# Router products and token-row turns moved into the loop of the mixer's output projection, with the norm applied per token at its end

## The reference, cut to what matters

```
def modulate(h, shift, scale):
    return h * (1.0 + scale) + shift
...
        x = x + g1 * mix
        h = modulate(rmsnorm(x, p['norm_ffn'][l]), sh2, sc2)
        x = x + g2 * hierarchical_moe(h, p['router_group_w'][l], p['router_group_b'][l],
...
    g_logits = (t @ wg + bg).astype(jnp.float32)
    g_idx = jnp.argmax(g_logits, axis=-1)
    e_logits = (jnp.einsum('nd,dge->nge', t, we) + be).astype(jnp.float32)
    e_val, e_idx = lax.top_k(e_in_group, TOP_K_IN_GROUP)
```

## Time and profile before

| | |
|---|---|
| median of 3 runs | 1279.28 us (1276.4 to 1279.57) |
| profiled execution, its own time | 1278.2 us |
| its span | 1276.4 us, 14669 instructions |
| TensorE busy | 1094.6 us (86%) |
| VectorE busy | 470.9 us (37%) |
| ScalarE busy | 257.2 us (20%) |
| GpSimd busy | 185.9 us (15%) |
| mean granted TensorE clock | 0.932 |
| read from and written to DRAM | 333.22 and 30.11 MB |

### The profile page before, as it was taken

The page is one execution under the profiler, slowest core; times in us unless marked ns, Lnnn a source line. Parts: engine busy times, 40 slices in busy tenths (PEclk is TensorE's granted clock), DMA queues, the critical chain, the costliest instruction groups (busy, mean ns, idle before and its releaser), DMA issues.

```text
span 1276.4 us, 14669 instructions
## 1 busy us (share of the span) xinstructions
PE 1094.6 (86%) x5453; PEld 577.4 (45%) x5453; DVE 470.9 (37%) x1002; ACT 257.2 (20%) x498; POOL 185.9 (15%) x209
## 2 busy tenths in 40 slices
PE   5799888987998889999789999989866988778865
PEld 3344555555443334443345565658752422222213
DVE  3356566134233112333363337792440111111116
ACT  3211344022333023323231110000221100000001
POOL 1020000002241113231100002130021222222100
PEclk9899999987999899999889999999877989989987
DMA  9996986432999559999960200505420899999933
GB/s 353 404 325 261 259 322 227 190 132 70 369 395 403 204 212 382 399 402 411 330 236 1 99 1 0 231 0 198 163 92 14 340 414 413 413 412 406 411 144 133
DMA packets 94241, 324.54 MB, mean 254 GB/s; under 512 B 17647, under 2 KB 33423, under 8 KB 77380
## 3 DMA queue, kind: packets, MB, share of 16 engines
q1 hardware_dynamic: 71936, 303.49, 61.4%
q0 software_dynamic: 15504, 13.37, 3.3%
q10 hardware_dynamic: 6708, 6.45, 1.4%
HBM read 333.22 MB, written 30.11 MB: 285 GB/s over the span
## 4 chain that ended last, share of the span: by engine, by line
PE 64%; DMA 19%; DVE 7%; issue 3%; ACT 3%; SPq 3%; POOL 0%; ACTq 0%; POOLq 0%; DVEq 0%
PE bank L844 15%; DMA ring<-in_moe_w_up 10%; PE bank L992 10%; PE bank L858 6%; PE bank L660 3%; PE bank L1031 3%; PE bank L776 3%; DMA ring<-in_w_ada 3%; DMA hT<-in_hy_log_decay 3%; PE bank L563 3%; PE bank L598 2%; PE bank L1020 2%; PE bank L978 2%; DMA ring<-in_moe_w_down 2%; PE bank L791 2%
## 5 line engine op out<-in xcount | busy, mean ns | idle before, releaser
L844 PE MATMUL bank<-ring,work 128*64 128x512 f32 x1120 | 268.9, 636 | 42.4 <-issue 36.3
L844 PEld LDWEIGHTS bank<-ring,work 128*64 128x64 f32 x1120 | 82.7, 146 | 220.0 <-issue 215.8
L858 PE MATMUL bank<-ring,work 128*64 128x512 f32 x560 | 129.2, 604 | 4.2 <-DVE work L1627 1.6
L992 PE MATMUL bank<-hT,ring 128*128 128x384 f32 x384 | 128.0, 494 | 5.3 <-ACT hT L1128 5.3
L1639 DVE SCALAR_TENSOR_TENSOR work<-bank,work 128x256 f32<-128x256 f32 x32 | 15.5, 484 | 261.0 <-ACT work L1224 261.0
L992 PEld LDWEIGHTS bank<-hT,ring 128*128 128x128 f32 x384 | 74.0, 194 | 58.0 <-issue 9.8
L858 PEld LDWEIGHTS bank<-ring,work 128*64 128x64 f32 x560 | 37.5, 138 | 74.0 <-issue 63.3
L1224 ACT ACTIVATE work<-bank 128x256 f32<-128x256 f32 x32 | 12.3, 384 | 247.5 <-PE bank L844 247.5
L1651 DVE COPY work<-bank 128x512 f32<-128x512 f32 x32 | 22.1, 692 | 106.5 <-PE bank L858 106.5
L1788 POOL DMA_INDIRECT work<-token_vectors,work x28 | 28.7, 1026 | 187.2 <-PE bank L827 172.5
L563 PE MATMUL bank<-ring,condS 128*32 128x256 f32 x768 | 47.0, 397 | 8.8 <-DVE ada L1328 5.5
(11 more groups left out here) (263 smaller groups left out, 1505.2 us busy)
## 6 DMA issues: line engine op xcount, KB each, us to landing
ring<-in_moe_w_gate SPq DMA_DIRECT2D x32, 2048.0 KB
ring<-in_moe_w_up SPq DMA_DIRECT2D x32, 2048.0 KB
ring<-in_moe_w_down SPq DMA_DIRECT2D x32, 2048.0 KB
ring<-in_w_ada SPq DMA_DIRECT2D x24, 2048.0 KB, 13.4
ring<-in_hy_w_in SPq DMA_DIRECT2D x6, 2048.0 KB, 19.8
filter_spectra<-work ACTq DMA_DIRECT2D x8, 768.0 KB
work<-expert_rows SPq DMA_DIRECT2D x16, 384.0 KB, 6.6
ring<-filter_spectra SPq DMA_DIRECT2D x2, 3072.0 KB, 12.0
```

The lines of the kernel that those rows point to most:

```text
L844: last = mm(bank[2][WIN * j:WIN * (j + 1), :], gt[:, k, WIN * j:WIN * (j + 1)], gu[:, :, j, k, :], start=(k == 0), stop=(k == KD - 1))
L858: last = mm(bank[b + hf][WIN * j:WIN * (j + 1), :], AT[:, k, WIN * j:WIN * (j + 1)], dn[:, j, k, hf * HALF:(hf + 1) * HALF], start=(k == 0 ...
L992: last = mm(bank[n % 2][:, 0:T], w[:, k, (n % 4) * P:(n % 4 + 1) * P], hT[:, k, :], start=(k == 0), stop=(k == KD - 1))
```

## The change

Several things are done together.

- In the projection's loop VectorE writes scale * x, without the norm, to hT for each finished block (router_x, xa_set). TensorE then forms the block's three router products, into one bank cleared by a product with zeros, and turns its three squares of 128x128 into banks 2, 5 and 6. Both come two blocks after the projection's own products, behind norm_sum. ScalarE copies the first half of the turned rows within the loop.
- The norm is applied per token afterwards: TensorE turns rstd with three one-column products, VectorE takes the reciprocal of 128x3 values and multiplies the logits; ScalarE scales the second half of a row as it copies it, and the first half in place (raw_rows).
- The shift's part of the logits comes from sums over the router's weights (shift_sums, shift_mm, shift_bias). For the token rows, the shift is turned to a row, written to DRAM and read back to all partitions by SyncE (shift_row), and added to hTok by GpSimd, one instruction of 128x1024 for each 128 tokens, which now count htok_set.
- The norm's products, the modulation and the separate stage of router products and turns go.
- ada_mm(11) goes from the attention loop to the place between layer 0's logits and masks; ada_mm(10) goes from head pair 5 to 6. The loads of pair 1's weights in layer 0 move behind pair 0's.
- In the router the count of extra windows and pair 1's one-hot come before the weights and the slot rows.
- GpSimd clears G after the first finished block; the square root's table is loaded before the squares; several semaphores are merged; layer 1's projection uses banks 0 and 1.

```diff
@@ -339,7 +344,7 @@
-        ADA_CORE = {0: 7, 2: 8, 4: 9, 5: 10, 7: 11}
+        ADA_CORE = {0: 7, 2: 8, 4: 9, 6: 10}
@@ -427,6 +433,14 @@
+        def shift_row(sp, l):
+            sp.wait_ge(sem("shift_set"), 2 * l + 2)
+            sp.dma_start(shD[l], strow).then_inc(sem("shrow_in"), 16)
+            sp.wait_ge(sem("shrow_in"), 48 * l + 16)
+            for c in range(2):
+                sp.dma_start(shrow[:, c, :].rearrange("p (k i) -> p k i", k=KD),
+                             shD[l].rearrange("(k c) i -> c k i", k=KD)[c].partition_broadcast(P)).then_inc(sem("shrow_in"), 16)
@@ -471,21 +485,22 @@
+            sp.wait_ge(sem("v_mm"), TC)
+            load_gu(sp, 0, 0, (0,))
+            shift_row(sp, 0)
+            sp.wait_ge(sem("mix_mm"), KD)
+            load_gu(sp, 0, 0, (1,))
+            load_dn(sp, 0, 0)
             sp.wait_ge(sem("ada_half"), 2 * NADA)
             load_gu(sp, 0, 1)
             load_dn(sp, 0, 1)
-            sp.wait_ge(sem("v_mm"), TC)
-            load_gu(sp, 0, 0, (0,))
-            sp.wait_ge(sem("mix0_mm"), KD)
-            load_gu(sp, 0, 0, (1,))
-            load_dn(sp, 0, 0)
@@ -622,9 +637,32 @@
+            def logit_mm(l, k):
+                if k == 0:
+                    pe.wait_ge(sem("rout_in"), 16 * 9)
+                pe.wait_ge(sem("xa_set"), 2 * (KD * l + k + 1))
+                if k == 0:
+                    mm(bank[4][:, 0:TC * (NG + NE)].rearrange("p (a b) -> p a b", a=4), ones, condS[:, 0:4, 2:29],
+                       start=True, stop=False, skip_group_check=True)
+                for c in range(TC):
+                    last = mm(bank[4][:, c * (NG + NE):(c + 1) * (NG + NE)], hT[:, k, c * P:(c + 1) * P], rout[:, l, k, :],
+                              start=False, stop=(k == KD - 1), skip_group_check=True)
+                if k == 4:
+                    pe.wait_ge(sem("hraw_set"), 9 * l + 3)
+                for c in range(TC):
+                    last = tr(bank[(2, 5, 6)[c]][:, k % 4 * P:(k % 4 + 1) * P], hT[:, k, c * P:(c + 1) * P], ident)
+                if k % 4 == 3:
+                    last.then_inc(sem("hraw_mm"), 1)
@@ -771,35 +807,31 @@
                 if m >= 2:
                     norm_sum(1, m - 2)
+                    logit_mm(0, m - 2)
...
-                pe.wait_ge(sem("rout_in"), 16 * 9)
-                for k in range(KD):
-                    wait_h(n_norm, k)
-                    for c in range(TC):
-                        last = mm(bank[c][:, 0:NG + NE], hT[:, k, c * P:(c + 1) * P], rout[:, l, k, :],
-                                  start=(k == 0), stop=(k == KD - 1))
-                last.then_inc(S_("logit_mm"), 1)
...
+                pe.wait_ge(sem("rt_done"), n_norm + 1)
+                for c in range(TC):
+                    last = mm(bank[3][:, c:c + 1], rstd[0:1, c * P:(c + 1) * P], ones[0:1, 0:1], start=True, stop=True)
+                last.then_inc(sem("row_mm"), 1)
+
+                if l == 0:
+                    pe.wait_ge(S_("lg_set"), B_("lg_set") + TC)
+                    ada_mm(NADA - 1)
@@ -1109,6 +1147,21 @@
+            def raw_rows(l, hf):
+                act.wait_ge(sem("hraw_mm"), 2 * l + hf + 1)
+                if hf == 1:
+                    act.wait_ge(sem("lg_set"), PER_LAYER["lg_set"] * l + 1)
+                for c in range(TC):
+                    rows = hTok[:, c, :].rearrange("p (k a) -> p a k", k=8)
+                    turned = bank[(2, 5, 6)[c]].rearrange("p (a k) -> p a k", k=8)
+                    if hf == 0:
+                        fn(rows[:, 0:64, :], turned, ACT.Copy).then_inc(sem("hraw_set"), 1)
+                    else:
+                        fn(rows[:, 64:128, :], turned, ACT.Identity, scale=rstdc[:, c:c + 1]).then_inc(sem("hraw_set"), 1)
+                        first = hTok[:, c, :].rearrange("p (k a) -> p k a", k=8)[:, :, 0:64]
+                        act.wait_ge(sem("hraw_set"), 9 * l + 3)
+                        fn(first, first, ACT.Identity, scale=rstdc[:, c:c + 1]).then_inc(sem("hraw_set"), 1)
@@ -1490,25 +1543,60 @@
+            def router_x(l, k):
+                dve.wait_ge(sem("mix_done"), 2 * (KD * l + k + 1))
+                for c, (lo, hi) in enumerate(SPANS):
+                    v.tensor_scalar(hT[:, k, lo:hi], xT[:, k, lo:hi], amul[:, l, 1, k, c:c + 1], None, ALU.mult)\
+                        .then_inc(sem("xa_set"), 1)
...
-                dve.wait_ge(S_("logit_mm"), B_("logit_mm") + 1)
+                dve.wait_ge(sem("row_mm"), 2 * l + 2)
+                link(v.reciprocal(rstdc, bank[3][:, 0:TC]))
+                dve.wait_ge(sem("hraw_mm"), 2 * l + 2)
@@ -1564,16 +1652,9 @@
-                dve.wait_ge(S_("gexp"), B_("gexp") + 2)
-                link(v.reduce_sum(gden, gx, axis=AX.X))
...
+                pair_rows(0)
+                if l == 0:
+                    ada_add(NADA - 1)
...
@@ -1768,8 +1863,14 @@
-                pool.wait_ge(sem(f"mix{l}_done"), 2 * KD)
+                pool.wait_ge(sem("mix_done"), 2 * KD * l + 2)
                 nc.gpsimd.memset(G.rearrange("p b d -> p (b d)"), 0.0).then_inc(S_("g_clear"), 1)
+                pool.wait_ge(sem("shrow_in"), 48 * (l + 1))
+                for c in range(TC):
+                    pool.wait_ge(sem("hraw_set"), 9 * l + 3 + 2 * (c + 1))
+                    row = hTok[:, c, :].rearrange("p (k a) -> p k a", k=8)
+                    shift = shrow[:, 1 if c else 0, :].rearrange("p (a k) -> p k a", k=8)
+                    nc.gpsimd.tensor_tensor(row, row, shift, ALU.add).then_inc(S_("htok_set"), 1)
                 nc.gpsimd.memset(Gx, 0.0).then_inc(S_("g_clear"), 1)
```

More of the change, by code:

```diff
@@ L167, in build @@
                 for l in range(DEPTH)]
+        shD = [nc.dram_tensor(f"shift_rows{l}", [2 * KD, P], F32, kind="Internal").ap() for l in range(DEPTH)]
         cfD = [nc.dram_tensor(f"filter_spectra{o}", [P, 6, D], F32, kind="Internal").ap() for o in range(2)]
@@ L325, in build @@
         m_all = small(TC, NE)
-        mtmp = [small(2, TC, NE) for _ in range(3)]
+        mtmp = [small(2, TC, NE) for _ in range(2)]
+        shacc, cbias = small(2, NG + NE), small(2, NG + NE)
+        rstdc = small(TC)
         posk, rowk, wck, basek, wink, rowq = [small(2, TC) for _ in range(6)]
@@ L624, in wait_h, with shift_mm @@
                 if k < H_ACT:
-                    pe.wait_ge(sem("h_act"), 2 * (H_ACT * n + k + 1))
+                    pe.wait_ge(sem("h_act"), 2 * (H_ACT * (n // 2) + k + 1))
                 else:
-                    pe.wait_ge(sem("h_dve"), 2 * ((KD - H_ACT) * n + k - H_ACT + 1))
+                    pe.wait_ge(sem("h_dve"), 2 * ((KD - H_ACT) * (n // 2) + k - H_ACT + 1))
+            def logit_mm(l, k):
[14 more added lines that the diff above has]
+                    last.then_inc(sem("hraw_mm"), 1)
+            def shift_mm(l):
+                pe.wait_ge(sem("shift_set"), 2 * l + 1)
+                for c in range(2):
+                    last = mm(bank[7][:, 64 * c:64 * c + NG + NE], ones, shacc[:, c, :], start=True, stop=True)
+                tr(bank[7][0:2 * KD, 256:256 + P], ada[:, l, 3].rearrange("p k c -> p (k c)"), ident).then_inc(sem("row_mm"), 1)
             for k in range(KD):
@@ L1552, in router, with pair_rows @@
                 link(v.tensor_tensor(rowk, rowk, wink, ALU.add))
-                for q in range(2):
+                def pair_rows(q):
                     r = rowk
@@ L1593, in router @@
                 v.tensor_copy(cumx[:, :], src_).then_inc(S_("cum_set"), 1)
+                pair_rows(1)
+                dve.wait_ge(S_("gexp"), B_("gexp") + 2)
+                link(v.reduce_sum(gden, gx, axis=AX.X))
+                link(v.tensor_scalar(den, ev, 1.0, None, ALU.add))
+                link(v.tensor_tensor(den, den, gden, ALU.mult))
+                link(v.reciprocal(wck[:, 0], den[:, :, 0]))
+                link(v.tensor_tensor(wck[:, 1], wck[:, 0], ev[:, :, 0], ALU.mult))
+                link(v.tensor_copy(idx[:, :], rowk.rearrange("p a b -> p (a b)")))
+                link(v.tensor_copy(pay[:, :, :, :].rearrange("p a b c -> p (a b c)"), trow[:, :]))
+                v.tensor_copy(pay[:, :, :, 2].bitcast(F32), wck).then_inc(S_("slots_set"), 1)
             def first(x, top, eq, key, oh, prio, n):
@@ L1603, in moe @@
                 S_, B_ = sem, lambda name: l * PER_LAYER[name]
-                norm(n_norm, l, 1)
                 router(l)
```

186 lines of the change are left out of this document (105 added, 81 removed).

## The result

The changed kernel takes 1282.17 us (median of 20 runs, 1278.05 to 1289.24) against 1277.84 us of the kernel before beside it (20 runs, 1275.26 to 1280.76): 1.0035 of its time, 95% interval 1.0023 to 1.0047. It is slower by 4.3 us, just over the 0.3% that can be told from no change; 1284.2 had been forecast. The profiled execution has a span of 1282.0 us against 1276.4.

A forecast was written before the change was run, and what follows sets the result against it. Mostly a serial order of TensorE matmuls (64% of the chain), with router stages as holes, was taken to bound the kernel. Terms of -1.0 us up to and in layer 0 and +5.9 in layer 1 gave 1279.3 + 4.9 = 1284.2 us, range 1270 to 1293.

The forecast's parts named there:

- attention: Attention loop: the twelfth conditioning product leaves it, 4.2 us gained (between 3.6 and 4.8).
- loop to first maximum, layer 0: Projection's loop to the router's first maximum in layer 0: router products and turns inside the loop gain 6.3 us.
- the same, layer 1: Projection's loop to the router's first maximum in layer 1: 6.9 us gained.
- stall by GpSimd's adds, layers 0 and 1: Router: VectorE's two-input instructions wait out GpSimd's three adds of 2.9 us each, +7.8 us in each layer.
- placement at the low clock, layers 0 and 1: Placement products after TensorE's idle time run at clock 0.50: +1.7 us in each layer, 0 without the drop.
- gather, layer 0: Layer 0's gather products start at the low clock as before and stay at 8.2 us (bounds 5.3 to 10.4).
- order at the router's end, layer 1: Count chain and pair 1's one-hot now stand before slots_set, which is on layer 1's path: +3.3 us.
- The forecast's base: The time of the kernel before to which the forecast added its +4.9 us: 1279.3 us.
- The prediction's list of signs: What would show it right, including a 6.8 us loop block and first maximum 12.2 us after the last output product.
- the faster rival: Router: no exclusion worth the name between GpSimd's adds and VectorE, both 7.8 us stalls gone, 1268.6 or 1265.2 us; chance 0.16.
- hidden, just: Layer 0's slot table, 3.7 us later, comes at 22.5 us, before pair 0's activation turn at 23.0 us: no cost.
- The weights moved behind pair 0: Layer 0's slot 1 loads start later, costed at nothing; rival that they bite: up to 5 us more, 1289 us, chance 0.07.

The follow-up runs named there:

- the fillers: Changed kernel plus unread TensorE products between logits and masks: 8 (layer 0) and 15 (layer 1), 1280.19 us, ratio 1.0009; earlier 12 and 26, 1288.6 us.
- the run with six adds: Changed kernel with GpSimd's shift added in six instructions of 512 columns in place of three of 1024: 1279.15 us, ratio 0.9986.

## Why the prediction was right, step by step

| step | forecast, us | profile of after | second profile |
|---|---|---|---|
| attention | -4.2 | -2.43 | -4.05 |
| loop to first maximum, layer 0 | -6.3 | -6.62 | -6.61 |
| the same, layer 1 | -6.9 | -7.21 | -7.21 |
| stall by GpSimd's adds, layers 0 and 1 | +7.8, +7.8 | +7.99, +7.85 | +7.96, +7.86 |
| placement at the low clock, layers 0 and 1 | +1.7, +1.7 | +1.58, +1.85 | +1.59, +1.86 |
| gather, layer 0 | 0 | -1.12 | -0.05 |
| order at the router's end, layer 1 | +3.3 | +2.83 | +2.91 |
| sum | +4.9 | +4.7 | +4.3 |

The second profile is the one of the changed kernel timed again beside the fillers. The agreement of the first column's sum is in part luck: attention gave 1.8 us less than forecast, and the gather 1.1 us and layer 1's order 0.5 us made up most of it. The last 0.9 us between the spans had no term. The forecast's base was also 1.4 us high, 1279.3 against 1277.8 in the longer series; the change was forecast as +4.9 us and measured as +4.3. The stall is the time from first maximum to masks less that of before, the placement VectorE's wait for it, the gather its 48 records (7.06 and 8.13 us, before 8.18; the granted clock over them was 0.78, 0.67 and 0.70), the order what is left of the last distance.

**The loop.** A block was forecast at 6.8 us and is 6.75. The last product ends at 273.72, and the first maximum starts 6.5 us later (6.3 by the forecast's 4.9 and 1.4). The prediction's list of signs has 12.2 us there; by its own sum that is the distance from the end of the old loop. That the router products run at the full clock in the loop holds (granted clock 1.00 from 241 to 270).

**The stall** was the term that decides, and it is shown: take away the adds' length, and the masks come 8.0 and 7.9 us sooner after the first maximum. From the two ways to pair 0 go 15.0 us, against the 15.6 of the faster rival; layer 0's placement at the full clock is in them. The add is 2.84 us for 2.9. The mechanism also holds at 24 columns, which no row of before showed: three instructions wait in each layer, each until a GpSimd add ends. One reading behind it was weaker than it was put: in all twelve cases of L1703 the recorded start of VectorE's instruction is 0.04 us ahead of GpSimd's, and the eight long ones are those that take their sign from the tile minus, the four short ones those with a constant. That GpSimd came in ahead was inferred from the lengths. L1359 shows it by the starts: the five long ones start 0.17 us after a GpSimd add. A small part had been left out: GpSimd's clear of Gx, behind the adds, holds L1610 for 0.85 us in place of 0.18. The Trainium skill (GPSIMD Engine Reference, Specifications) says that GpSimd's interfaces to SBUF are shared with VectorE, with contention for instructions that have two SBUF inputs or run in a 2-port mode. The trace agrees, and adds the price: the VectorE instruction waits out the whole GpSimd instruction, and the reductions don't wait. The 3.3 us that the prediction estimated for the add from the Trainium skill (GPSIMD Engine Reference, Performance pitfalls for Q7 kernels) is too high here: 2.84 us, with 0.51 us for the stride.

**The placement** ran at a granted clock of 0.50 (1.2 of 2.4 GHz) as forecast. That it is the clock and not the instruction is shown by the fillers in layer 1: 2.2 us in place of 4.1. VectorE's wait was 3.41 us in both layers, 1.83 and 1.56 before. Layer 0, before and after:

```profile
296.69 0.42 DVE L1544 TENSOR_TENSOR work<-bank,work 128x96 f32<-128x96 f32 x2 [1.83 <-PE bank L808]
```

```profile
297.67 0.42 DVE L1632 TENSOR_TENSOR work<-bank,work 128x96 f32<-128x96 f32 x2 [3.41 <-PE bank L840]
```

**The attention term** is the one that was mis-sized, 4.2 against 2.4 in the profiled execution. The product that left the last head pair had covered a wait of TensorE for ScalarE of 0.9 us. Without it the granted clock falls there in some executions. Stretches of the changed kernel in the first profile and in the second: length, PE, PEld, DVE, ACT, POOL busy, PEclk, DMA share, GB/s.

```profile
215.00:219.40 4.40, 4.25 (x24) 2.67 (x24) 1.69 (x6) 0.60 (x1) 0.00 (x0) 0.61 0.05 20
```

```profile
215.00:219.40 4.40, 3.71 (x34) 2.64 (x36) 2.62 (x7) 1.41 (x3) 0.00 (x0) 1.00 0.03 9
```

At the full clock the distance is 37.33 us and the gain 4.05, at the low one 38.95 and 2.4. Of the eleven profiles with this schedule four show the fall, always with the same 1.6 us (of the first eight also four, not three as the expectation counted). The two profiles with the product in its old place (before, and the run that puts it back) show no fall. Two are too few to show that the product had prevented it, so this cause is likely and not shown. The forecast took the product's length and its wait as the gain, which holds at the full clock, and did not ask what the product kept running.

**The order** costs 2.8 and 2.9 us in layer 1. In layer 0 it stays hidden at pair 0, with nothing to spare. GpSimd's first read by the table is at 321.31; VectorE's product of pair 0's activation, which also reads the table, ends at 322.73, and TensorE's turn of it follows at 322.79, in its old place behind the gather products. But the first profile's chain goes over the slot table and GpSimd's gathers to pair 3, where TensorE waits 0.78 us. The gather's gain of 1.1 us is spent there. Before, and after:

```profile
362.74 7.09 PE L844 MATMUL bank<-ring,work 128*64 128x512 f32 x32
```

```profile
363.61 7.26 PE L877 MATMUL bank<-ring,work 128*64 128x512 f32 x32 [0.78 <-issue]
```

In the second profile there is no such wait. From the first maximum to this point both take 83.4 us, against 74.0 before. So "hidden, just" holds only as long as layer 0's gather is slow.

**The weights moved behind pair 0** bite nowhere: no wait of pair 1 for its slot, as forecast.

## What to carry to other kernels

Work moved to GpSimd to take it off the path can be on it all the same: if VectorE works through a chain of small instructions, each that meets a GpSimd instruction may wait out the whole of it; which ones do is shown below. Before such a move, look for a place where VectorE waits for another engine; here the same adds on VectorE, inside its wait for the placement, cost little. When an instruction leaves an engine, ask what it covered, and whether it may have kept TensorE's clock up in a wait. When a stage gets shorter, look again at what was hidden behind it, here the slot table.

## What the hardware showed unexpectedly

- TensorE's clock fell with hardly any idle time before it. In the first profile of the changed kernel TensorE had been idle for 0.96 us after a run of products of 36 columns and of one column; the granted clock was 0.73 (1.2 GHz for a part of it) in the microsecond from 280 and 0.52 from 281 to 284, though the conditioning product (5.35 us from 280.21) was running. In the second profile the same product ran in full speed, 3.66 in place of 5.35 us. Before, router products ran from 277.88 on for 10.4 us without a gap, and the clock stayed at 0.50.
- An add of 128x1024 on VectorE takes 1.95 us with one operand at a stride of eight values and 1.17 us without; on GpSimd it is 2.84 and 2.33 us.
- Which VectorE instruction waits depends on both sides. GpSimd's adds hold up two-input instructions and L1610, which has one input and a scalar (1.44 us in the run with six adds). GpSimd's clear (memset) of 0.95 us holds up L1610 as well, 0.85 us in place of 0.18. But two-input instructions keep their length beside it (0.18 us in the run with six adds, shown here), and reductions wait for neither (0.18 us):

```profile
289.74 0.95 POOL L1877 MEMSET work<- 128x1024 f32 x1
290.09 0.18 DVE L1689 TENSOR_TENSOR work<-work 128x24 f32<-128x24 f32 x1
```
